# Two transformer blocks in fp32 on one core: a new order of the first stages, triangular inverses on four corners of the array, and shorter chains behind two recurrences

## What is computed

```python
# block 1
h = rms_norm(x, norm1_g); proj = h @ w_in
p_rwkv, p_sb, q_mem, gate_logits = split(proj)
# rwkv7, 8 heads of 64, for each token t:
#   S = S * w_t + (S @ -kk_t) x (kk_t * a_t) + v_t x k_t ;  y_t = S @ r_t
# kk = kk / |kk|;  y = (y - mean) * rsqrt(var + eps) * lnx_g + lnx_b
# y_a = (y + sum(r * k * r_k) * v) * g
y_a = rwkv7_branch(p_rwkv, ...)
y_b = stick_breaking_branch(p_sb, ...)         # 8 heads of 64, 2 query blocks of 128
y_m = memory_branch(q_mem, mem, ...)           # 4 heads of 128, 256 memory rows
merged = sum over n of sigmoid(gate_logits[n]) * (ys[n] @ w_branch[n])
x = x + merged @ w_out
x = x + conv_ffn(x, ...)                       # 1024 -> 2 x 2816 -> 1024
# block 2
x = x + mlstm(rmsnorm(x)) @ w                  # 4 heads, q and k 128, v 256, per-head norm, gate
x = x + ffn(x); x = x + moba_attention(x); x = x + ffn(x)
```

## Time and profile before

| | before |
|---|---|
| median of 3 runs | 1228.22 us (1227.84 to 1228.34) |
| the profiled execution's own time | 1228.64 us |
| its span | 1226.8 us |
| PE busy | 1170.8 us (95%) |
| DVE, ACT, POOL busy | 900.0, 659.8, 370.9 us |
| read from HBM | 186.52 MB |

### The profile page before, as it was taken

One profiled execution on the slowest core, in us unless ns is written; L12 is line 12 of the kernel. 1 busy time (PEld: TensorE's weight loads), 2 busy tenths in 40 slices (PEclk: granted clock), 3 DMA queues, 4 the chain that ended last, 5 costly groups with the idle time before them and its releaser, 6 DMA issues.

```text
span 1226.8 us, 24693 instructions
## 1 busy us (share of the span) xinstructions
PE 1170.8 (95%) x9392; PEld 1086.7 (89%) x9392; DVE 900.0 (73%) x1298; ACT 659.8 (54%) x966; POOL 370.9 (30%) x330
## 2 busy tenths in 40 slices
PE   6998998999999999999998999999999989999998
PEld 6986778989999999988887899998898789999987
DVE  6977646446568988866667688887676758888863
ACT  4676862335445555543557466555454665555542
POOL 6533102000002555511202335552146123455500
PEclk9999999999999999999999899999999999999999
DMA  8643210135556555555543455555554415555562
GB/s 291 223 134 120 87 52 3 37 104 189 185 168 226 174 175 178 181 188 173 163 151 99 137 165 181 175 184 180 186 170 143 134 66 175 173 176 176 176 187 71
DMA packets 53987, 188.77 MB, mean 154 GB/s; under 512 B 6032, under 2 KB 6160, under 8 KB 53520
## 3 DMA queue, kind: packets, MB, share of 16 engines
q1 hardware_dynamic: 52304, 182.47, 46.1%
q10 hardware_dynamic: 1600, 5.12, 1.2%
HBM read 186.52 MB, written 1.05 MB: 153 GB/s over the span
## 4 chain that ended last, share of the span: by engine, by line
PE 78%; DVE 10%; ACT 6%; issue 3%; POOL 2%; DMA 1%; ACTq 0%; DVEq 0%; SPq 0%; POOLq 0%
PE psA L460 68%; PE psB L460 10%; DVE rounded L1721 3%; DVE arena L1724 3%; ACT arena L1122 3%; DVE arena L1721 2%; ACT L1122 2%; ACT rounded L1122 2%; POOL arena L1544 1%; POOL arena L1559 1%; DMA arena<-in_x 1%; DVE arena L2055 0%; POOL rounded L1651 0%; DVE arena L2104 0%; DVE arena L2202 0%
## 5 line engine op out<-in xcount | busy, mean ns | idle before, releaser
L460 PE MATMUL psA<-rounded,rounded 128*128 128x256 f32 (+1 forms) x7440 | 1016.3, 298 | 35.0 <-DVE rounded L1721 16.3
L460 PEld LDWEIGHTS psA<-rounded,rounded 128*128 128x128 f32 x7440 | 960.1, 193 | 85.9 <-issue 20.5
L1721 DVE TENSOR_TENSOR rounded<-arena,rounded 128x1024 fp32r<-128x1024 f32 (+3 forms) x358 | 452.3, 1284 | 74.4 <-ACT rounded L1122 70.4
L1122 ACT ACTIVATE rounded<-arena 128x1024 fp32r<-128x1024 f32 (+2 forms) x442 | 388.4, 923 | 197.2 <-PE psA L460 66.0
L1544 POOL TENSOR_TENSOR arena<-arena 128x256 f32<-128x256 f32 (+1 forms) x123 | 162.1, 1324 | 595.6 <-ACT arena L1122 224.8
L1122 ACT ACTIVATE arena<-arena 128x256 f32<-128x256 f32 (+8 forms) x273 | 143.7, 561 | 187.7 <-DVE arena L1721 133.7
L1724 DVE SCALAR_TENSOR_TENSOR arena<-arena 128x255 f32<-128x255 f32 (+4 forms) x334 | 177.4, 575 | 37.6 <-ACT arena L1122 28.3
L460 PE MATMUL psB<-arena 64*64 64x64 f32 (+11 forms) x1816 | 153.2, 271 | 11.9 <-DVE arena L1721 6.9
L460 PEld LDWEIGHTS psB<-arena 64*64 64x64 f32 (+5 forms) x1816 | 112.3, 149 | 42.5 <-issue 25.3
L1721 DVE TENSOR_TENSOR arena<-arena,psA 128x256 f32<-128x256 f32 (+1 forms) x84 | 38.4, 457 | 71.7 <-PE psA L460 47.8
L1636 POOL TENSOR_TENSOR rounded<-arena,rounded 128x256 f32 (+1 forms) x63 | 76.7, 1218 | 10.6 <-POOL rounded L1634 9.4
(11 more groups left out here) (70 smaller groups left out, 166.8 us busy)
## 6 DMA issues: line engine op xcount, KB each, us to landing
arena<-in_w SPq DMA_DIRECT2D x343, 512.0 KB, 3.5
arena<-in_mem ACTq DMA_DIRECT2D x2, 512.0 KB, 7.2
arena<-in_x ACTq DMA_DIRECT2D x1, 1024.0 KB, 6.2
arena<-in_con ACTq DMA_DIRECT2D x1, 1024.0 KB, 6.3
out<-arena SPq DMA_DIRECT2D x1, 1024.0 KB, 3.9
arena<-in_con ACTq DMA_DIRECT2D x1, 992.0 KB, 6.8
arena<-in_w SPq DMA_DIRECT2D x2, 256.0 KB, 3.1
arena<-in_x SPq DMA_DIRECT2D x2, 256.0 KB, 5.6
```

The source lines that it names most:

```text
L460: ins_ = nc.tensor.matmul(o, l, r, start=start, stop=stop, skip_group_check=shared)
L1122: return nc.scalar.activation(o, i, f, **kw)
L1721: return V.tensor_tensor(o, a, b, op)
```

## The change

The diff does four things. Line numbers shift, since new code comes ahead of the helpers: mm is L460 before and L483 after, the DVE subtraction L1721 before and L1878 after, the ACT helper L1122 before and L1253 after.

**1. First stages.** Twelve idle matmuls on a blanked buffer come ahead of rw0; rw2 comes ahead of the sum of squares `rx`; every split in this stretch stands one or two slots earlier in the DVE and ACT programs; in the chain that makes the scan's factors (kk, decays), single splits stand between the 1024-wide products; the score rows of `z` have no splits between them any more; ACT loads the table for Sqrt with a dummy operation; the products `BN=(BN+lb)*GT` and `GT*=lg` are made here instead of behind the scan.

```diff
+            idle_products(12)
             project(["rw0"], (xgH, xgL), "xg")
-            project(["rw1"], (xgH, xgL))
+            project(["rw1", "rw2"], (xgH, xgL))
             pe.wait_ge(sem("ld_con"), 16)
             sum_squares("rx", "x", sqx)
-            project([f"rw{u}" for u in range(2, 7)], (xgH, xgL))
+            project([f"rw{u}" for u in range(3, 7)], (xgH, xgL))
...
-            split_to(7)
+            split_to(8)
             dve.wait_ge(*freed("rx"))
             step(V.reciprocal(rstd, rstd))
...
             split_to(SLOT_END["mv1"])
+            dve.wait_ge(*freed("gl1"))
+            for c in range(4):
+                mark(stt(BN[:, c, :], BN[:, c, :], pcol("lb", c), GT[:, c, :], ALU.add, ALU.mult))
+            settle()
+            for c in range(4):
+                mark(V.tensor_scalar(GT[:, c, :], GT[:, c, :], pcol("lg", c), None, ALU.mult))
```

```diff
-            for l in range(1, 6):
-                for g in range(2):
-                    o = open_(f"l{l}p{g}")
-                    pe.wait_ge(*freed(f"l{l - 1}x{g}"))
-                    close(chunks(o, lower(g), at(X, g)), f"l{l}p{g}")
+            corners = ((0, 0), (1, 1), (0, 1), (1, 0))
+            def order(g, corner):
+                at = [[(a, i) for i in range(8 * g, 8 * g + 8) for a in range(2) if corner(a, i) == c] for c in corners]
+                return [q for k in range(8) for cell in at for q in cell[k:k + 1]]
...
+            branch(0, range(0, 2))
             for l in range(1, 6):
                 for g in range(2):
+                    level_factor(l, g)
+                if l == 1:
+                    for g in range(2):
+                        first_inverse_t(g)
+                branch(*FILL[2 * l - 2])
+                if l < 5:
+                    for g in range(2):
+                        level_inverse(l, g)
                 for g in range(2):
+                    level_inverse_t(l, g)
+                branch(*FILL[2 * l - 1])
```

```diff
+            split_to(SLOT_END["br%d.%d" % BR[5]] + 2)
+            ready(dve, "y_sq", 2)
+            mark(tt(YT, YT, GT, ALU.mult))
+            settle()
             ready(dve, "y_inv")
-            step(tt(YT, YT, YQ, ALU.mult))
-            split_to(SLOT_END["br%d.%d" % BR[6]] + 2)
-            for c in range(4):
-                mark(V.tensor_scalar(YT[:, c, :], YT[:, c, :], pcol("lg", c), pcol("lb", c), ALU.mult, ALU.add))
-            settle()
-            step(tt(YT, YT, BN, ALU.add))
-            merge(6)
-            tt(ys[:, 0:4, :], YT, GT, ALU.mult).then_inc(sem("ys"), 1)
...
+            for u in range(2):
+                c = slice(2 * u, 2 * u + 2)
+                tt(ys[:, c, :], YT[:, c, :], BN[:, c, :], ALU.add).then_inc(sem("ys"), 1)
+            split_to(SLOT_END["br%d.%d" % BR[6]] + 1)
```

```diff
-            project_first("aw0", (hrH, hr), "hr_rest", 2)
-            project([f"aw{u}" for u in range(1, 4)], (hrH, hr))
+            project_two(("aw0", "aw1"), (hrH, hr), "hr_rest", 2)
+            project([f"aw{u}" for u in range(2, 4)], (hrH, hr))
...
+def project_two(names, src, wait, per):
+                for j in range(4):
+                    for k in range(4):
+                        if j == 0:
+                            ready(pe, wait, k // per + 1)
...
+                for j in range(4):
+                    for k in range(4, KD):
+                        if j == 0:
+                            ready(pe, wait, k // per + 1)
```

More of the change, by code:

```diff
@@ L796, in unit_, with branch @@
-            def unit_(h, i):
-                return ident[h, h]
-            for g in range(2):
+            def branch(u, ks=range(KD + W4)):
+                m, n = BR[u]
+                name = f"br{m}.{n}"
+                o = bank(name) if ks[0] else open_(name)
+                for k in ks:
+                    if k < KD:
+                        last = mm3(o[:, 0:T], weights(1), part(H, slice(0, P), k), k == 0, k == KD - 1)
+                        continue
+                    if k == KD and u in (0, 1, 2 * KD):
+                        ready(pe, "ys_split", min(u, 2) + 1)
+                    elif k == KD + 2 and u == 2 * KD:
+                        ready(pe, "ys_split", 4)
+                    last = mm3(o[:, T:2 * T], weights(1), part((YH, ys), slice(0, P), n * W4 + k - KD),
+                               k == KD, k == KD + W4 - 1)
+                if ks[-1] == KD + W4 - 1:
+                    close(last, name)
@@ L799, in _, with first_inverse, first_inverse_t @@
+            def first_inverse(g):
                 o = open_(f"l0x{g}")
                 ready(pe, "LT", 4 * g + 4)
-                close(chunks(o, lower(g), unit_), f"l0x{g}")
-            for g in range(2):
+                for a, i in order(g, lambda a, i: (a, a)):
+                    last = mm(tile(o, a, turned_half(1, i), 0, among(1, i)), lower(a, i),
+                              ident[halves[a], halves[a]], True, True)
+                close(last, f"l0x{g}")
+            def first_inverse_t(g):
@@ L823, in _ @@
                 o = open_(f"ut{t}")
-                pe.wait_ge(*freed(f"l5t{t}"))
+                for g in range(2):
+                    pe.wait_ge(*freed(f"l5t{g}"))
                 pe.wait_ge(*freed(f"tr{t}.a"))
@@ L2004, in merged_rest @@
                 tt(fr(mg[:, m, :]), mg[:, m, :], rd(mgH[:, m, :]), ALU.subtract).then_inc(sem("merged_rest"), 1)
[L2005 removed]
+            for u in range(6, 3 * KD):
                 merge(u)
```

343 lines of the change are left out of this document (223 added, 120 removed).

## The result

| | before | after |
|---|---|---|
| median, same chip | 1228.28 us | 1201.32 us (1200.54 to 1202.52, 4 runs) |
| ratio, 95% interval | | 0.9782 (0.9765 to 0.9799) |
| profiled execution, its span | 1228.64, 1226.8 us | 1200.83, 1198.8 us |

The account below looks back on a forecast made before the run. PE was taken as the bound, busy 1170.8 of 1226.8 us. Terms -11.4 - 14.5 - 2.9 - 6.0 = -34.8 against 1228.64 give 1193.8; 1.5 added for slacks that may fail gives 1195, range 1186 to 1209.

Parts of the forecast that it names:

- the likeliest case: Whole kernel: all four parts gain about as summed, 1195 us, own range 1190 to 1199, chance 0.60.
- two rivals: Levels: corners run no deeper, 1205 to 1209 us (0.15). First stages: waits come back, 1201 to 1203 us (0.13).
- First stages: PE's stalls from 8.46 to 136 us and a clock fall, 15.2 us, go, less new waits: -11.4, from -6 to -13.6.
- the new waits at slots 9 and 10: First stages, behind rx: PE waits about 1.9 and 0.9 us for splits, +2.8 against 3.3 that go.
- The fall of the clock: First stages: the 0.50 clock for 3.4 us behind the 2.64 us stall goes with it, worth 1.7 us.
- The slacks that the prediction names: First stages: replayed splits of the scan's factors are ready only 0.4 to 0.7 us early; failing, the part gains 6.
- Levels: 64x64 products: four corners -14.0, a stall -3.1, tile switches +2.2, copies at ut +0.4; sum -14.5, bounds -0.5 and -16.
- I take 0.467 for the 30 groups: Levels: with four corners a group of 32 records takes 0.467 us instead of 0.935, -14.0 us.
- each corner takes its next record 60 ns behind its last: Levels: two corners start together, each taking its next about 60 ns later, so four corners fit four records, 0.467 a group.
- Scan and norm: Behind the scan: a 2.68 us wait and its half clock, 4.4 us, go; waits of 1.1 and 0.35 come: -2.9.
- mLSTM's end: A 7.22 us wait and 2.5 of half clock go, waits of 1.95 and 1.2 come: -6.0, from -3 to -8.
- +0.6 for a fall of the clock: mLSTM's end: the clock may still fall at the new waits, costing 0.6 us of the part's gain.

Follow-up runs that it names:

- old_splits: The changed kernel with the old places of the splits and the old DVE and ACT order from the scan's factors to z: 1212.57 us, ratio 0.9872.
- before_with_end: The kernel before with only the fourth part of the change, the mLSTM's end: 1222.64 us, ratio 0.9945.
- no_pieces: The changed kernel with 22 of the 24 blocks of branch units 0 and 1 put behind the last level instead of between its groups: 1206.16 us, ratio 0.9805.
- no_idle_products: The changed kernel without the twelve idle products and the memset ahead of them: 1205.42 us, ratio 0.9805.
- one_corner: The changed kernel with a group's products in corner order, four in a row on one corner, then four on the next: 1219.32 us, ratio 0.9916.
- pieces_cut: The changed kernel with every matmul of the pieces (branch units 0 and 1) cut into two of 128 columns: 1204.97 us, ratio 0.9791.
- two_corners: The changed kernel with each group's products going first round corners (0,0) and (1,1), then (0,1) and (1,0): 1203.28 us, ratio 0.9779.
- aw_one_tile: The changed kernel with PE's old order of aw at the mLSTM's end, the vector engines' order staying changed: 1205.17 us, ratio 0.9806.
- changed_again: The changed kernel itself, unedited, run once more on another occasion: 1202.45 us, ratio 0.9778; its profile is of its slowest run, 1205.22 us.
- changed_old_end: The changed kernel with the mLSTM's end as before on all engines: 1206.49 us, ratio 0.9809.

## Why the prediction was right, and where it was off

The sign and the range held; the sum was 6 us too large, and the levels, forecast as the largest part by 3 us, came out just under the first stages. The 1201.3 lie outside the likeliest case's own 1190 to 1199. They are inside the range because it was widened for two rivals, neither of which happened: the groups did get faster, and no first-stage stall of over 2 us came back. Luck helped too: 2.4 us came from a stage where nothing was forecast and nothing changed. By its steps:

- **First stages, -11.4 forecast, -9.6 measured.** The replay of DVE's order held: all seven stalls around the factors and z went, but for two waits of 0.57 (old_splits brings the seven back), and the new waits at slots 9 and 10 were 2.4 for 2.8. The fall of the clock went as well, but old_splits didn't bring it back with its stall, so its 1.7 us hang on more than the places of the splits. What failed is a chain that the sum leaves out: DVE and ACT work through the stick-breaking chain (rows of 1536 columns, 1.5 us each on ACT) from 115.65, and PE, no longer held up by splits, comes to the products that need it 1.7 us too early. The slacks that the prediction names are at the splits of the factors; for this chain it has only the 0.6 of short waits.
- **Levels, -14.5 forecast, -9.3 in the first profile, and only -6 to -8 in four others of the same code** (levels 35.0, 35.6, 36.5 and 37.5 us). All this is against the one profile of before, 34.3; the same old code took 36.9 in before_with_end, so single profiles give this part no better than to 2 or 3 us. The step "I take 0.467 for the 30 groups" held: 0.467 is what a group between two others takes. At a piece it is more, 0.51 behind it and 0.58 to 0.62 ahead of it, and a piece itself takes 0.19 beyond its matmuls (6 of them 0.91 for 0.72). With both borders that is some 0.37 a piece, about 4 us for 11 pieces, where the sum had 2.2. The copies at ut made PE wait 1.08, not 0.4. The largest miss, 2.4 us here and 2.8 to 4.1 in seven other traces with these levels, is a bound that the sum didn't have: instructions come in loads of 16 KB, each worth 126 matmuls with their weight loads, and where PE waited at both ends, a load took 3.55 us at the least (207.89 to 211.44) and up to 4.2. The levels of the changed kernel hold 8.7 loads, so with 3.55 us each they take some 31 us (an estimate), and they took 33.8 to 37.5. Before, 126 matmul records were nearly four groups, 3.7 us, so the same bound lay just under the old rate and didn't show. no_pieces shows it plainly, no_idle_products that the waits move with the count of instructions, and one_corner and pieces_cut that they go when PE is slower.
- **Which mechanism made groups faster.** The prediction reasoned that each corner takes its next record 60 ns behind its last. two_corners (0.59 a group) and one_corner (1.15, not 1.9) contradict that simple rule, so that it gave the right 0.467 for four corners is partly luck. That the order of corners sets the rate is shown (0.47, 0.59, 1.15 between two groups, with equal instructions); what exactly held the old loop at 0.935 is open. The rule of the Trainium skill that was set against it ("TensorE: Matmul & The Clock Gate", section "Wait — 56ns, not 53.3ns?", no start sooner than about 25 ns behind another) would have made groups 0.80; 32 records in 0.467 us are 14.6 ns each, so the measurement decides against it for 64x64 tiles on four corners. On the switches the Trainium skill's page "TensorEngine Tiling (Array Packing)" says in its section "Key Properties" that changing the tiling mode drains the engine; the 0.19 us a piece agree in kind.
- **Scan and norm, -2.9 forecast, -2.4 measured**, with a wait of 1.32 for 1.1. About half of this is the clock that fell behind the old stall in the profile of before; in before_with_end it didn't, and the same old code took 1.2 us less.
- **mLSTM's end, -6.0 forecast, -4.7 measured.** The two waits came 0.2 to 0.5 us shorter than replayed. Not seen was the wait of 1.18 behind the two units. That the two passes hold four slots at once, so that the slot behind them is split late, would explain it, but isn't shown (aw_one_tile). That kernel also shows that PE's two passes are worth 3.6 us of the part. The +0.6 for a fall of the clock wasn't needed in this profile, but it fits: in changed_again, where the clock does fall here, the part takes 0.6 us more.
- **The last stage, 0 forecast, -2.4 measured.** In the kernel before, 800 matmuls of the last loop take 100.5 us, in the changed one 98.1, in all other kernels here 98.1 too:

```profile
1064.00:1076.00 12.00, 11.96 (x98) 11.58 (x97) 10.61 (x17) 6.74 (x11) 6.98 (x7) 1.00 0.53 175
```

```profile
1038.00:1050.00 12.00, 12.00 (x100) 11.82 (x99) 10.77 (x17) 7.12 (x11) 6.57 (x7) 1.00 0.52 175
```

In the slow rhythm POOL's cast starts 0.2 us behind a DVE split and takes 1.26 us. In the quick one it starts 0.07 ahead of the split and takes 0.40, and the split takes 1.41 in place of 1.22:

```profile
1063.12 1.22 DVE L1721 TENSOR_TENSOR rounded<-arena,rounded 128x1024 fp32r<-128x1024 f32 x1
1063.33 1.26 POOL L1634 CAST rounded<-arena 128x256 f32 x1 [0.17 <-POOL arena L1544]
```

```profile
1037.44 0.40 POOL L1793 CAST rounded<-arena 128x256 f32 x1 [0.17 <-POOL arena L1708]
1037.51 1.41 DVE L1878 TENSOR_TENSOR rounded<-arena,rounded 128x1024 fp32r<-128x1024 f32 x1
```

The two traces agree to 0.02 us up to the loop's first turn, where one ACT instruction starts 0.3 us later in the kernel before. It hangs on none of the parts, since before_with_end and changed_old_end both have the quick one; why only the kernel before falls into the slow one stays open, and there is only one profile of it. So in the two profiles 2.4 of the 28 us are luck, as far as the runs show, and 25.7 come from the four parts.

## What to carry to other kernels

Stalls that are only places of splits can be replayed from the trace to a few tenths, but each one taken away brings the engine sooner to the next chain: look for what has under 2 us of slack behind it. Where many tiny matmuls run faster than before, count instructions, not only array time: the branch work between the levels, with few instructions and long rows, cost 5.2 us less there than behind them in the two profiles (33.8 against 39.05 us with the same 8.7 us of work), and some 4 us in the medians (1201.3 and 1202.5 against 1206.16). A gain of 1 us in such a stretch can't be measured against loads that arrive differently in each run. And a fall of the clock behind a stall isn't a fixed price: the same stalls had it in one trace and not in another.

## What was not expected of the hardware

- A load of instructions (16 KB, 126 matmuls and 126 weight loads) took 3.55 to 4.2 us where PE waited for it in the levels at full clock, and PE stood still for 0.2 to 2.1 us at its end, in the middle of a group. With the wait the clock sometimes fell to 0.50 for 3.4 or 6.8 us.
- A matmul of the rounded format with 128 columns took 0.11 us (worked out from 12 in a row, 1.48 us less 0.19), one with 256 columns 0.12.
- 64x64 products of equal number took 0.47, 0.59 or 1.15 us a group of 32 records by the order of the corners alone (after, two_corners, one_corner).
